# Value products of a dilated attention with the roles of weights and activations swapped

## What is computed

```python
kv = (_rms(x, kv_norm) @ w_kv).reshape(bsz, seq, 2, B_GROUPS, B_HEADS, B_HEAD_DIM)
k = _rms(kv[:, :, 0], k_gain[:, None, :])
v = kv[:, :, 1]
q = _rms((h @ w_q).reshape(...), q_gain) * (B_HEAD_DIM ** -0.5)
# for each group: masked scores with a relative bias, softmax, then
o = jnp.einsum('bhrij,bjrhd->birhd', p, vb)
# and a softmax over the groups' log-sum-exp weighs the three outputs
return o @ w_o
```

## Time and profile before

| | |
|---|---|
| median of 3 runs | 2557.44 us (2553.1 to 2557.51) |
| profiled execution, its own time | 2556.5 us |
| its span, first to last instruction | 2554.7 us |
| TensorE busy, weight loads busy | 97%, 95% of the span |
| VectorE busy, ScalarE busy | 68%, 52% |
| mean granted clock of TensorE | 0.995 |
| dilated stage | about 2055 to 2355 us |

### The profile page before, as it was taken

How to read it: one execution, slowest core, us unless ns; L and a number is a source line. 1 busy time by engine, 2 the same in 40 slices (tenths; PEclk the granted TensorE clock), 3 DMA queues, 4 the chain that set the end, 5 groups by cost and what they waited for, 6 DMA issues and landing times.

```text
span 2554.7 us, 60487 instructions
## 1 busy us (share of the span) xinstructions
PE 2489.3 (97%) x23329; PEld 2423.8 (95%) x23329; DVE 1744.9 (68%) x2871; ACT 1316.9 (52%) x1997; POOL 79.0 (3%) x122
## 2 busy tenths in 40 slices
PE   8998998999999999999999999899999999999999
PEld 8997977989999999989999999899999999999999
DVE  6757677567766757767766767967667666666774
ACT  5534444455545546555545547455455455555552
POOL 0000442000000000000000000000000000000000
PEclk9999999999999999999999999999999999999999
DMA  6663301435655656445655655246656665553664
GB/s 203 218 211 125 100 12 44 149 126 181 208 185 188 212 202 185 153 136 182 207 181 188 211 176 190 75 126 201 203 173 201 200 188 153 157 157 111 195 210 136
DMA packets 119840, 425.14 MB, mean 166 GB/s; under 512 B 16673, under 2 KB 24564, under 8 KB 119412
## 3 DMA queue, kind: packets, MB, share of 16 engines
q1 hardware_dynamic: 111616, 411.65, 49.7%
q10 hardware_dynamic: 8052, 11.04, 2.3%
HBM read 421.51 MB, written 1.12 MB: 165 GB/s over the span
## 4 chain that ended last, share of the span: by engine, by line
PE 87%; DVE 5%; ACT 3%; issue 2%; POOL 1%; SPq 0%; DMA 0%; ACTq 0%; DVEq 0%; POOLq 0%
PE bank L492 20%; PE bank L487 20%; PE bank L491 20%; PE bank L410 5%; PE bank L415 4%; PE bank L414 4%; ACT hi L348 1%; PE bank L2410 1%; DVE lo L356 1%; PE bank L468 1%; PE bank L470 1%; PE bank L469 1%; PE bank L1812 1%; PE bank L1785 1%; PE bank L1797 1%
## 5 line engine op out<-in xcount | busy, mean ns | idle before, releaser
L356 DVE TENSOR_TENSOR lo<-raw,hi 128x1024 fp32r<-128x1024 f32 (+1 forms) x728 | 935.3, 1293 | 381.0 <-ACT hi L348 379.2
L348 ACT ACTIVATE hi<-raw 128x1024 fp32r<-128x1024 f32 (+1 forms) x728 | 782.2, 1106 | 292.9 <-PE bank L415 168.1
L487 PE MATMUL bank<-Hh,hi 128*128 128x256 f32 x3024 | 836.3, 277 | 3.1 <-DVE lo L356 2.0
L492 PE MATMUL bank<-Hh,lo 128*128 128x256 f32 x3024 | 837.4, 277 | 0.0
L491 PE MATMUL bank<-Hl,hi 128*128 128x256 f32 x3004 | 830.1, 276 | 0.0
L487 PEld LDWEIGHTS bank<-Hh,hi 128*128 128x128 f32 x3024 | 567.9, 188 | 4.3 <-DVE lo L356 4.0
L492 PEld LDWEIGHTS bank<-Hh,lo 128*128 128x128 f32 x3024 | 568.1, 188 | 0.0
L491 PEld LDWEIGHTS bank<-Hl,hi 128*128 128x128 f32 x3004 | 564.3, 188 | 0.0
L487 PE MATMUL bank<-Ah,hi 128*128 128x256 f32 x1408 | 389.7, 277 | 1.9 <-DVE lo L356 1.9
L492 PE MATMUL bank<-Ah,lo 128*128 128x256 f32 x1408 | 390.1, 277 | 0.0
L491 PE MATMUL bank<-Al,hi 128*128 128x256 f32 x1400 | 387.2, 277 | 0.0
(11 more groups left out here) (445 smaller groups left out, 4042.3 us busy)
## 6 DMA issues: line engine op xcount, KB each, us to landing
raw<-in_w SPq DMA_DIRECT2D x600, 512.0 KB, 3.7
raw<-in_w SPq DMA_DIRECT2D x128, 704.0 KB, 4.9
dB<-dil_bias ACTq DMA_DIRECT2D x16, 384.0 KB, 10.4
X<-in_x SPq DMA_DIRECT2D x2, 512.0 KB, 5.9
mem_x<-in_mem ACTq DMA_DIRECT2D x2, 512.0 KB, 4.4
gWS<-in_ws ACTq DMA_DIRECT2D x1, 1024.0 KB
gBS<-in_bs ACTq DMA_DIRECT2D x1, 1024.0 KB
out_x<-X SPq DMA_DIRECT2D x4, 256.0 KB, 2.6
```

What stands on the lines that cost most here:

```text
L348: act.activation(k.hi[:, q, :w], k.raw[:, q, :w], ACT.Copy).then_inc(k.hi_ready, 1)
L356: dve.tensor_tensor(k.lo[:, q, :w], k.raw[:, q, :w], k.hi[:, q, :w].bitcast(F32), ALU.subtract).then_inc(k.lo_ready, 1)
L487: pe.matmul(out, wh, xh, start=first, stop=False)
L492: mm = pe.matmul(out, wl, xh, start=False, stop=last)
```

## The change

The value slabs are computed with the roles swapped: the activations (128 tokens of one input chunk) are stationary and the slab's weights (128 columns) move. The 256 tokens make two halves, so a value slab has 8 x 2 x 3 = 48 matmuls of 128 columns, each with its own load, where it had 24 of 256. The result stands as tokens by features. The factor 1/rms is then one per partition: two small products in chunk 0 turn the row into columns `RC`, and ScalarE copies each half to `VT` with it as its scale. The value transposes, VectorE's multiplies and the tensor `VF` go. ScalarE now releases the value banks, at positions 7 (two of them) and 8, and VectorE waits for its last release before it empties the first bank of the next chunk.

```diff
@@ pe @@
+                elif x == "v":
+                    self.pe_value_slab(pe, s)
...
-                if c and i == 2:
-                    self.pe_values(pe, c - 1)
...
+                if c == 0 and i == 4:
+                    for half in range(2):
+                        ins = pe.matmul(k.bank[7][:, 12 + 2 * half:14 + 2 * half], k.RKV[:, half * P:(half + 1) * P],
+                                        k.ident[:, 0:2], start=True, stop=True)
+                    k.pe_done.done(ins, "d.rc")
@@ the tail @@
-        self.pe_values(pe, last)
+        k.dve_done.wait(pe, f"d.add{last}.1")
@@
-    def pe_values(self, pe, c):
...
-                ins = pe.transpose(out, self.VF[:, g, half * P:(half + 1) * P], k.ident)
-        k.pe_done.done(ins, f"d.vt{c}")
+    def pe_value_slab(self, pe, s):
+
+        k, q = self.k, s % RING
+        pe.wait_ge(k.lo_ready, s + 1)
+        pe.wait_ge(k.banks_freed, RING + s - 2)
+        for kc in range(NC):
+            wh, wl = (w[:, q, kc * P:(kc + 1) * P] for w in (k.hi, k.lo))
+            for half in range(2):
+                out = self.bank(s)[:, half * P:(half + 1) * P]
+                xh, xl = (x[:, kc, half * P:(half + 1) * P] for x in (k.Kh, k.Kl))
+                pe.matmul(out, xh, wh, start=kc == half == 0, stop=False, skip_group_check=True)
+                pe.matmul(out, xh, wl, start=False, stop=False, skip_group_check=True)
+                ins = pe.matmul(out, xl, wh, start=False, stop=kc == NC - 1, skip_group_check=True)
+        ins.then_inc(k.slab_used, 1)
@@ pe_output @@
-        k.act_done.wait(pe, f"d.vt{c}")
+        k.act_done.wait(pe, f"d.vt{c}.2")
@@ act @@
-                if c and i == 2:
-                    self.act_values(act, c - 1)
+                if c == 0 and i == 6:
+                    k.pe_done.wait(act, "d.rc")
+                    d(act.activation(self.RC[:].rearrange("p h n -> p (h n)"), k.bank[7][:, 12:16], ACT.Copy), "d.rc")
...
+                if i == 7:
+                    self.act_values(act, c, 0)
+                    self.act_values(act, c, 1)
+                if i == 8:
+                    self.act_values(act, c, 2)
@@
-        k.act_done.done(act.activation(flat[:, :512], first[:], ACT.Copy), f"d.vt{c}")
-        k.act_done.done(act.activation(flat[:, 512:], rest[:, :T], ACT.Copy), f"d.vt{c}")
+    def act_values(self, act, c, g):
+
+        k, s = self.k, self.slab(c, "v", g)
+        act.wait_ge(k.slab_used, s + 1)
+        act.wait_ge(k.banks_freed, RING + s)
+        if c:
+            k.pe_done.wait(act, f"d.o{c - 1}.0")
+        else:
+            k.act_done.wait(act, "d.rc")
+        for half in range(2):
+            ins = act.activation(self.VT[:, half, g, :], self.bank(s)[:, half * P:(half + 1) * P], ACT.Copy,
+                                 scale=self.RC[:, half, 0:1])
+            k.act_done.done(ins, f"d.vt{c}.{g}")
+        k.act_done.wait(act, f"d.vt{c}.{g}")
+        act.sem_inc(k.banks_freed, 1)
@@ dve @@
-                dve.wait_ge(k.slab_used, s + 1)
...
-                    ins = dve.tensor_tensor(self.VF[:, g, :], bank, k.RKV[:], ALU.mult)
+                if x != "v":
+                    if c and i == 0:
+                        dve.wait_ge(k.banks_freed, RING + s)
+                    dve.wait_ge(k.slab_used, s + 1)
```

More of the change, by code:

```diff
@@ L1610, in __init__ @@
         self.QSQ = k.at("dQSQ", a + 18 * KB, [P, GROUPS, T])
-        self.VF = k.at("dVF", a + 21 * KB, [P, GROUPS, T])
         self.VT = k.at("dVT", a + 24 * KB, [P, 2, GROUPS, P])
@@ L1617, in __init__ @@
         self.RR = k.at("dRR", a + 38 * KB, [P, T])
+        self.RC = k.at("dRC", a + 39 * KB, [P, 2, 2])
         self.B = [k.at(f"dB{z}", (86 + 6 * z) * KB, [P, 2, GROUPS, T]) for z in range(2)]
@@ L1652, in turned_banks @@
         return ((3, 4), (4, 2)) if c < NC - 1 else ((4, 4), (5, 2))
-    def value_banks(self, c):
-        return 6, 3 if c < NC - 1 else 7
     def block(self, half, e, j):
@@ L1792, in pe_transposes @@
         k.dve_done.wait(pe, f"d.p{c}.{half}")
-        k.act_done.wait(pe, f"d.vt{c}" if half else f"d.pt{c}.1")
+        if not half:
+            k.act_done.wait(pe, f"d.pt{c}.1")
         places = [(b, j) for b, n in self.turned_banks(c, half) for j in range(n)]
@@ L1859, in act @@
                     self.act_heads(act, c - 1)
+                if i == 7:
[3 more added lines that the diff above has]
+                    self.act_values(act, c, 2)
         last = NC - 1
         self.act_exp(act, last, 1)
-        self.act_values(act, last)
         self.act_exp(act, last, 0)
@@ L1956, in dve @@
                     k.act_done.wait(dve, "d.rr")
-                dve.wait_ge(k.slab_used, s + 1)
[L1958 to L1963, removed]
-                    ins = dve.tensor_tensor(self.VF[:, g, :], bank, k.RKV[:], ALU.mult)
[L1965 to L1968, removed]
+                if x != "v":
+                    if c and i == 0:
+                        dve.wait_ge(k.banks_freed, RING + s)
+                    dve.wait_ge(k.slab_used, s + 1)
+                    bank = self.bank(s)[:, :T]
+                    if x == "k":
+                        ins = dve.tensor_tensor(self.K[z][:, g, :], bank, k.RKV[:], ALU.mult)
+                    else:
+                        ins = dve.tensor_tensor(self.Q[z][:, g, :], bank[:, ::-1], self.RR[:], ALU.mult)
+                    ins.then_inc(k.banks_freed, 1)
+                    if g == GROUPS - 1:
+                        dve.wait_ge(k.banks_freed, RING + s + 1)
+                        d(dve.engine_nop(), {"k": f"d.kraw{c}", "q": f"d.qraw{c}"}[x])
                 if i == (7 if c else 4):
```

## The result

The changed kernel took 2610.17 us (median of 4 runs, 2610.02 to 2613.34), the kernel before 2557.48 (median of 4). The ratio is 1.0215, 95% interval 1.0203 to 1.0227: slower by 52.7 us. The forecast was slower, 2614, range 2604 to 2630.

A forecast was written before the change was run, and what follows sets the result against it. TensorE's gap-free instruction queue was taken to bound the dilated stage. Slabs +61.9, transposes -5.3, norm column +0.4 and tail +0.2 made +57.2 us on 2556.5 or the median 2557.44, so 2614, range 2604 to 2630.

The forecast's parts named there:

- The price of a narrow pair: Value slabs: a full 128-column load with 128 columns streamed costs 0.112 us, bounds 0.108 and 0.118, set by the load.
- The two-column and parted rows: Profile rows before: two-column query sums at 0.110 to 0.113 us a pair, a 192/64-column float32r product at 0.110 each.
- Point 1: Value slabs: a block goes from 8.79 to 16.53 us, +7.74, uncovered; +61.9 us over eight blocks.
- Point 2: Value transposes: six per block go, 0.66 us on the chain, -5.3 us over eight blocks.
- Point 3: Block 0: two small float32 products turn the 1/rms row into columns, four pairs on the chain, +0.4 us.
- Points 4 to 7: VectorE's lost multiplies and new wait, ScalarE's changed copies, later bank release, weight ring: each worth 0 on TensorE's chain.
- Point 8: Tail, last block: only about 0.5 of the transposes' 0.66 us can come back there, so +0.1 to +0.2 us.
- The sum: All terms on TensorE's chain: 61.9 - 5.3 + 0.4 + 0.2 = +57.2 us.
- A pair cheaper than its load: Rival, value slabs: a pair costs 0.059 us at most, about -6 us, so 2551; 3%.
- a free repeat of a load: Rival, value slabs: second load of the same activations skipped, pairs 0.075 us each, +14, so 2571; 6%.
- slow narrow float32r: Rival, value slabs: products under 256 columns run as float32 in two passes, +186 us, so 2742; 4%.
- The 2%: Rival's chance: the clock falls to its 1.2 GHz level in the value slabs, pairs 0.194 us, +151, so 2708.

The follow-up runs named there:

- the transposes alone: Kernel before with only two of the six value transposes of a block done: 2551.8 us beside 2555.1, ratio 0.9988, stage 3.8 us shorter.
- the split: Kernel before, weights stationary and transposes kept, each value-slab product done in two pieces of 128 columns: 2617.9 us beside 2557.7, stage +61.7 us.

## Why the prediction was right, point by point

- *The bound.* TensorE's queue sets the stage, and what is added to it is added to the time: shown by the equal growth of TensorE's busy time and of the span, and in the small by the transposes alone.
- *The price of a narrow pair.* 0.112 was forecast, 0.1117 measured. That the load sets it is shown by halving the load (0.061 to 0.063) and by narrowing the stream at full clock (0.11). The two-column and parted rows were the right neighbours.
- *Point 1.* A block's value slabs 16.33 us for 16.53 forecast, +7.54 for +7.74 by the chain's rows; by block, 42.64 - 35.62 = +7.02 for +7.08. The restart of 0.2 us after narrow products is 0.15 in these slabs (5.51 against 5.36).
- *Point 2.* The transposes were on the chain: -3.8 us for four of six, and 4.9 between the split and the swapped kernel, for 5.3.
- *Point 3.* The two small products took 0.45 us in the chain (at 2073.33), for 0.4.
- *Points 4 to 7, worth 0.* No new wait of TensorE, beyond 0.2 us ahead of the first key sums. ScalarE's copies of 128 columns were cheaper than their bound:

```profile
2179.00 1.06 ACT L348 ACTIVATE hi<-raw 128x1024 fp32r<-128x1024 f32 x1 [3.64 <-PE bank L1755]
2179.96 0.61 ACT L1923 ACTIVATE dVT<-bank,dRC 128x128 f32<-128x128 f32 x2
```

  They end at 2180.57, and VectorE empties the next query bank at 2185.90: 5.3 us of cover, five forecast.
- *Point 8.* The last small scores and the next transposes of probabilities in the chain, before and after:

```profile
2339.32 0.94 PE bank L1785 x12
...
2346.60 1.32 PE bank L1797 x12
```
```profile
2396.43 0.94 PE bank L1786 x12
...
2403.23 1.54 PE bank L1799 x12
```

  From start to start 7.28 us became 6.80: the 0.5 of the 0.66 that the prediction allowed came back. Then 0.22 of it was lost again in the transposes, 1.54 us instead of 1.32, so the tail gave back 0.26.
- *The sum.* +57.2 against +56.8 in the stage. The chain divides it: +7.9 in block 0 (8.1 forecast), 7 x 7.02 in the blocks behind it (7 x 7.08), -0.26 in the tail (-0.5). So the errors of the terms are tenths and partly cancel. The 2610.2 of the result lies 4 us under the forecast, which is within the spread of few runs; five further runs gave 2613.3. That they came so near to 2614 is in part luck.
- *The rivals.* A pair cheaper than its load, and a free repeat of a load, are refuted by the changed kernel's own load rows; slow narrow float32r by them too. The clock did not fall with 128 columns. The 2% was too little thought for it, though: at 96 and 64 columns it fell, and no row of before had shown it. The argument given against it, that the changed slabs bring no wait, doesn't hold in general: the clock fell without a wait. The grams, which were cited for it, are less like the value slabs than they look: a float32 instruction of 256 columns costs 1.29/6 = 0.215 us in the key sums, where a float32r pair of 256 costs 0.114 to 0.118, so a gram's columns aren't streamed as those of a value slab are. That the clock held at 128 was forecast rightly, but on thin grounds.

## What to carry to other kernels

Price a stream of matmuls by the larger of its load and its stream, here 0.112 us for 128 loaded columns against 0.118 for 256 moving and 0.175 for 384; a change of roles that halves the moving columns doubles the loads and so the time, whatever transposes it saves. Count what it saves in the same coin: six transposes were six pairs, the split added 72. If the roles must be swapped, let several slabs move behind one load, and look whose queue releases what they hold.

## What the runs showed that was not expected

- In a gap-free stream of full loads with 64 columns each the granted clock fell to 0.50; with 96 columns it was 0.65 on average over 20 us, with 128 columns it stayed 1.00, and so it did with loads of 64 columns and 128 streamed. At 0.50 a pair that waits only for its load costs 0.213 us instead of 0.112, so work left out made the kernel 100 us slower. Why the clock fell stays open.
- The stage was the same within 0.1 us in two executions of the changed kernel, while its start moved by 4 us. For a change inside such a stage one trace of each kernel tells tenths of a microsecond, where the medians of four runs were 4 us off.
